# Hybrid trunk on one core: masks made early, fewer VectorE lines per HGRN head, and the S5 half of an output projection in portions between the levels

## The reference

```python
proj = hn @ w_in_even[j]
u, q_b, f_b, i_b, g_b = jnp.split(proj, ...)
y_a = s5_mixer(u, ...)            # gelu, then z * sigmoid(z @ w_glu + b)
y_b = hgrn2_mixer(q_b, f_b, i_b, g_b, lower_bounds[j], hgrn_norm[j])
h = h + jnp.concatenate([y_a, y_b], axis=-1) @ w_out_even[j]

# hgrn2_mixer, per head, in chunks of 64 tokens
k = (1.0 - lbf) * jax.nn.sigmoid(-zf)
b = jnp.cumsum(g_c, axis=2)                     # log decays
o = (q*exp(b)) @ S + (causal q.decay.k) @ v
S_new = exp(b_last) * S + (k*exp(b_last - b)).T @ v
o = o * rsqrt(mean(o*o) + EPS) * head_norm * silu(g)
```

## Time and profile before

| quantity | value |
|---|---|
| median of 3 runs | 2602.95 us (2598.78 to 2605.69) |
| the profiled execution | 2599.74 us |
| its span | 2598.0 us |
| mean granted TensorE clock | 0.971 |
| busy: PE, PEld, DVE, ACT, POOL | 95%, 77%, 46%, 21%, 32% of the span |
| head 0 / heads 1, 2, 3 / last tail | 338 to 378.6 / 378.6 to 465.8 / 465.8 to 484.5 us |
| output projection | 484.5 to 574.8 us |

### The profile page before, as it was taken

One profiled execution on the slowest core, in us unless ns is written; L12 is line 12 of the kernel. 1 busy time (PEld: TensorE's weight loads), 2 busy tenths in 40 slices (PEclk: granted clock), 3 DMA queues, 4 the chain that ended last, 5 costly groups with the idle time before them and its releaser, 6 DMA issues.

```text
span 2598.0 us, 32798 instructions
## 1 busy us (share of the span) xinstructions
PE 2464.0 (95%) x13054; PEld 1998.5 (77%) x13054; DVE 1191.4 (46%) x1229; ACT 548.1 (21%) x850; POOL 833.8 (32%) x493
## 2 busy tenths in 40 slices
PE   8999946899999999999997999989999999999997
PEld 6887745688888888888885776668888888888885
DVE  6886388432432422424617355652432332424625
ACT  3110424311001011011212145632001001011215
POOL 3421442133333333333322244552333333333321
PEclk9999967999999999999998999999999999999998
DMA  7372421211111111111212211021111111111211
GB/s 209 101 115 73 144 68 34 98 49 49 49 48 48 46 46 48 47 48 48 65 49 85 53 25 57 17 73 49 49 46 47 47 47 48 48 48 49 65 49 65
DMA packets 248296, 159.19 MB, mean 61 GB/s; under 512 B 31524, under 2 KB 235400, under 8 KB 248200
## 3 DMA queue, kind: packets, MB, share of 16 engines
q1 hardware_dynamic: 233224, 133.79, 17.9%
q10 hardware_dynamic: 14992, 24.25, 3.5%
HBM read 131.67 MB, written 25.17 MB: 60 GB/s over the span
## 4 chain that ended last, share of the span: by engine, by line
PE 86%; DVE 9%; issue 2%; ACT 2%; POOL 1%; DMA 0%; ACTq 0%; POOLq 0%; DVEq 0%; SPq 0%
PE ps L596 70%; PE ps L1075 3%; PE ps L747 2%; PE ps L1107 2%; PE ps L1035 1%; DVE hg_queries_keys L1849 1%; PE ps L1048 1%; PE ps L1059 1%; PE ps L663 1%; PE ps L768 1%; DVE stage L1519 1%; ACT x_hi L1158 1%; PE ps L783 1%; DVE s_state L1589 1%; DVE stage L1589 1%
## 5 line engine op out<-in xcount | busy, mean ns | idle before, releaser
L450 POOL CAST w_hi<-w_raw 128x1024 fp32r<-128x1024 f32 x198 | 213.0, 1076 | 1499.6 <-PE ps L596 1222.5
L596 PE MATMUL ps<-x_hi,w_hi 128*128 128x512 f32 x1600 | 496.6, 392 | 6.4 <-issue 3.2
L596 PE MATMUL ps<-x_lo,w_hi 128*128 128x512 f32 x1600 | 493.3, 389 | 0.0
L596 PE MATMUL ps<-x_hi,w_lo 128*128 128x512 f32 x1600 | 493.0, 389 | 0.0
L452 POOL TENSOR_TENSOR w_lo<-w_raw,w_hi 128x1024 fp32r<-128x1024 f32 x198 | 487.7, 2463 | 15.8
L596 PE MATMUL ps<-mid_hi,w_hi 128*128 128x512 f32 x1216 | 376.1, 391 | 8.6 <-DVE mid_lo L1908 5.8
L596 PE MATMUL ps<-mid_lo,w_hi 128*128 128x512 f32 x1216 | 375.3, 390 | 0.0
L596 PE MATMUL ps<-mid_hi,w_lo 128*128 128x512 f32 x1216 | 375.2, 390 | 0.0
L596 PEld LDWEIGHTS ps<-x_hi,w_hi 128*128 128x128 f32 x1600 | 299.9, 188 | 73.2 <-issue 8.8
L596 PEld LDWEIGHTS ps<-x_lo,w_hi 128*128 128x128 f32 x1600 | 300.7, 188 | 62.9
L596 PEld LDWEIGHTS ps<-x_hi,w_lo 128*128 128x128 f32 x1600 | 300.6, 188 | 62.7
(11 more groups left out here) (288 smaller groups left out, 2488.7 us busy)
## 6 DMA issues: line engine op xcount, KB each, us to landing
w_raw<-w_mlp_in_in SPq DMA_DIRECT2D x64, 512.0 KB, 4.0
w_raw<-w_mlp_out_in SPq DMA_DIRECT2D x64, 512.0 KB, 4.0
w_raw<-w_in_even_in SPq DMA_DIRECT2D x20, 512.0 KB, 4.0
residual_dram<-residual ACTq DMA_DIRECT2D x2, 4096.0 KB, 13.0
fqig_dram<-stage ACTq DMA_DIRECT2D x16, 512.0 KB, 2.7
w_raw<-w_ple_gate_in SPq DMA_DIRECT2D x16, 512.0 KB, 4.0
x_tokens<-x_in SPq DMA_DIRECT2D x8, 512.0 KB, 7.3
w_raw<-w_out_even_in SPq DMA_DIRECT2D x8, 512.0 KB, 4.1
```

The costliest lines, as they stand in the source:

```text
L450: pool.tensor_copy(WH[:, b, :], RAW[:, b, :]).then_inc(S["w_hi_done"], 1)
L596: ins = pe.matmul(acc[:, h, :], w[:, k, :], x[:, k0 + k, h * HALF:(h + 1) * HALF], start=(k == 0 and w is wh and x is xh), stop=(k == kts ...
```

## The change

- **Masks.** GpSimd makes them right behind slab 3, in a staging buffer, with the same instructions (the block mask as a fifth plane). ScalarE's queue stores them to DRAM; SP loads the diagonal blocks and the block mask back, 5 small DMAs, behind the S5 outputs. `near_masks` only clears `ATD` and waits.
- **Fewer VectorE lines.** `keys` is gone: ScalarE multiplies the keys by `keep`, and the token factor of the values is applied by `value_copy`, now four activations of 128x128 with a per-partition scale (eight small transposes beside the S5 preparation make it a column). `mean_square` is gone: ScalarE's Ln reads PSUM with scale and bias. `near` is 4 instructions of both halves, `attend` 1 per half. For that, banks are dealt anew: near 4, 5; direct 6, 7; transposes and squares both share bank 2, so each waits for the copy of the one before.
- **S5 half first.** The output projection is split by depth. The S5 half (192 matmuls of 512 columns) runs through bank 3 as 16 portions of 12 matmuls. After each of the 14 slots of `hd` = 1 to 4 TensorE runs `FILL` = 4 of them, until they are spent (slot 5 of `hd` = 4). Before portion j it waits for ScalarE's copy of portion j-1. ScalarE copies each at a fixed place of its list (`parts`) and stores it to DRAM. Four slabs of 512 KB with half the depth and twice the width feed it, split by GpSimd behind each head's work.
- **After the heads.** SP restores the residual and the stored part tile by tile, 16 DMAs of 512 KB, 8 MB in all, and only then loads slabs 28 and 29. GpSimd adds the part to the residual (`add_out_part`), three tiles before slab 28, two before slab 29, three after it. The HGRN half runs as 8 units of 24 matmuls.

```diff
             for s in range(2, 4):
                 one(s, s - 1)
-            run(4, 4, 16)
-            one(20, 19)
-            pool.wait_ge(S["s5_y_done"], 8)
+            pool.wait_ge(S["sumsq_ready"], 1)
             own(pool.memset(FULL[:, :, :], 1.0))
...
+            run(4, 4, 16)
+            one(20, 19)
             one(21, 20)
...
+                if hd:
+                    one(SLAB["out"] + hd + 1, 4 * hd, "opart_done")
+            one(SLAB["out"] + 5, 16, "opart_done")
+            def add_out_part(m):
+                pool.wait_ge(tile_loaded[m], 16 * 3)
+                pool.tensor_tensor(H[:, m, :], H[:, m, :], OPART[:, m, :], ALU.add).then_inc(S["out_part"], 1)
+            for m in range(KT):
+                add_out_part(m)
+                if m in (2, 4):
+                    one(SLAB["out"] + 5 + m // 2, UNIT["out"] + m, "acc_done")
...
+            for b in range(2):
+                sp.wait_ge(spilled[b], 16 * (10 + KT))
+            for m in range(KT):
+                sp.dma_start(H[:, m, :], h_dram[m * P:(m + 1) * P, :]).then_inc(tile_loaded[m], 16)
+                sp.dma_start(OPART[:, m, :], part_dram[m * P:(m + 1) * P, :]).then_inc(tile_loaded[m], 16)
+            out_half(1, 2)
+            out_half(1, 3)
...
+            def out_first():
+                pe.wait_ge(S["mid_ready"], 8)
+                for m in range(KT):
...
+                    for h in range(2):
+                        if m + h:
+                            pe.wait_ge(S["opart_copied"], 2 * m + h)
+                        for k in range(4):
+                            for w, x in ((wh, XBh), (wh, XBl), (wl, XBh)):
+                                ins = pe.matmul(PS[:, 3, :], ...)
+                                yield
...
                         if now:
                             level(hd, l, half)
+                        if hd:
+                            dense(first, FILL)
...
-                fn(KQ[:, p, 1, half * HALF:(half + 1) * HALF], FR[:, p, half, :], ACT.Sigmoid, scale=-1.0)
+                own(fn(k, FR[:, p, half, :], ACT.Sigmoid, scale=-1.0))
+                fn(k, k, ACT.Identity, scale=keep[:, hd:hd + 1])
...
+            def parts(hd, slot):
+                while copied[0] < 2 * KT and 12 * (copied[0] + 1) <= FILL * (2 * LEVELS * (hd - 1) + slot + 1):
+                    j = copied[0]
+                    act.wait_ge(S["opart_done"], j + 1)
+                    fn(o, PS[:, 3, :], ACT.Copy).then_inc(S["opart_copied"], 1)
+                    act.wait_ge(S["opart_copied"], j + 1)
+                    act.dma_start(part_dram[...], o).then_inc(spilled[m % 2], 16)
...
+            for hd in range(1, HEADS + 1):
+                key_copy(tail, 0)
+                parts(hd, 0)
+                key_copy(tail, 1)
+                if now:
+                    gate(hd)
+                parts(hd, 5)
+                if hd < HEADS - 1:
+                    for half in range(2):
+                        forget(hd + 1, half)
+                parts(hd, 6)
+                for half in range(2):
+                    squares(tail, half)
+                    if now:
+                        value_copy(hd, half)
+                    parts(hd, 8)
+                act.preload_act_table_set("natural_log_exp_and_others")
+                for half in range(2):
+                    head_rstd(tail, half)
+                    parts(hd, 10 + half)
+                if now:
+                    direct_copy(hd, 0)
+                    parts(hd, 12)
+                    direct_copy(hd, 1)
+                parts(hd, 13)
+                for half in range(2):
+                    y_high(tail, half)
...
             def block_decays(hd):
+                dve.wait_ge(S["hg_f_made"], 2 * hd + 2)
```

More of the change, by code:

```diff
@@ L41 @@
 LAG = 2
+FILL = 4
 V_STEP = 12
@@ L903, in _ @@
             pe.wait_ge(S["mid_ready"], 8)
-            one(22, 24, XB)
-            one(23, 25, XB)
-            run(24, 26, 6, XB)
+            pe.wait_ge(S["opart_copied"], 16)
+            for m in range(KT):
+                u = UNIT["out"] + m
+                if m % 2 == 0:
+                    pe.wait_ge(S["w_ready"], SLAB["out"] + 4 + m // 2 + 1)
+                pe.wait_ge(*free_of(u - 2))
+                wh, wl = out_weights(m)
+                unit(ACC[m % 2], wh, wl, XBh, XBl, kts=4, k0=4)
             def mlp(name, norm, mid0):
@@ L1111, in wo_first @@
                                 yield
-            def dense(work, count):
-                for _ in range(count):
-                    next(work, None)
             pe.wait_ge(S["ss_read"], 4)
@@ L1373, in _ @@
                     if now:
-                        gate(hd)
-                    if hd < HEADS - 1:
-                        for half in range(2):
-                            forget(hd + 1, half)
-                    for half in range(2):
-                        squares(tail, half)
-                        if now:
-                            value_copy(hd, half)
-                    act.preload_act_table_set("natural_log_exp_and_others")
-                    for half in range(2):
-                        head_rstd(tail, half)
-                elif HEADS > 1:
-                    for half in range(2):
-                        forget(1, half)
@@ L1394, in _ @@
+                if now:
+                    direct_copy(hd, 0)
+                    parts(hd, 12)
+                    direct_copy(hd, 1)
+                parts(hd, 13)
+                for half in range(2):
+                    y_high(tail, half)
+            assert copied[0] == 2 * KT
             finish(1, "mlp", 0)
@@ L1914, in _ @@
             for half in range(2):
-                keys(0, half)
                 query_decay(0, half)
@@ L1942, in _ @@
                         if l == 3:
-                            for half in range(2):
-                                near(hd, half)
+                            near(hd)
                     if hd == 0:
@@ L1957, in _ @@
                             forget_in(nxt, half)
-                    if hd and l in (4, 5):
-                        mean_square(tail, l - 4)
                     if nxt < HEADS and l == 4:
-                        for half in range(2):
-                            keys(nxt, half)
                         block_decays(nxt)
@@ L2057, in embed @@
                 end_norm()
[L2059 to L2060 removed]
+            for b in range(2):
+                dve.wait_ge(spilled[b], 16 * (10 + KT))
+            residual(UNIT["out"], 1, ("mlp", 0), None, parts=True)
             mlp("mlp0", 1, 8, (2, ("ple", 0)))
```

171 lines of the change are left out of this document (101 added, 70 removed).

## The result

The changed kernel takes 2614.0 us, median of 5 runs (2609.97 to 2617.53), against 2598.8 us for the kernel before on the same chip: a ratio of 1.0048, 95% interval 1.0031 to 1.0066. It is slower by half a per cent, where 0.6% faster was forecast. The profiled execution took 2617.53 us (span 2615.7), which is 17.7 us of span above the one of before.

The account below looks back on a forecast made before the run. TensorE alone was taken to bound the output projection, a relay with VectorE the fuller partner the heads. +1.0 - 4.2 + 0.7 + 20.0 + 1.0 - 35.3 = -16.8 us gave a median of 2586 us, range 2563 to 2603.

Parts of the forecast that it names:

- start, GLU slab, head 0: Ahead of head 1: masks +1, second GLU slab without its wait -4.2, head 0 +0.7 us; together -2.5.
- heads 1 to 3: Heads 1 to 3 with portions: 35.4, 38.3 and 33.7 us, 107.4 for 87.2, so +20 us.
- last tail: Tail behind the heads: portions and shared bank 2 cost, one VectorE hop goes; +1 us (0 to +5).
- output projection: Output projection with half its matmuls, a 6.5 us slab stall ahead of unit 4: 90.3 becomes 55.0, -35.3 us.
- with the portions it is 30.4 ... so TensorE becomes the bound: Heads 1 to 3: TensorE's own 17.7 us a head becomes 30.4, above all VectorE sums, so TensorE bounds them.
- Waits for bank 3: Heads 1 to 3: TensorE waits for ScalarE's portion copies, 5.0, 7.9 and 3.3 us by head.
- the upper end: Heads 1 to 3: every wait half as long again and a half clock after the long ones, +32 us.
- GpSimd's splits slow VectorE's two-input lines: In the heads: four GpSimd splits of 3.4 us each slow VectorE, inside the ends given, with TensorE the bound.
- pays nothing there: Heads 1 to 3: VectorE's removed lines, about 5 us a head, save nothing because TensorE is the bound.
- The lower-clock one: Rival: bank waits keep TensorE at its lower clock through the heads; heads and tail +68, 2633 us; chance 9%.
- It decides from +46 on: Heads and tail: from +46 us on, the result counts for the rival of TensorE's lower clock level, chance 9%.
- The third: Rival: worse waits, or VectorE and TensorE alternate instead of overlapping; heads and tail +34, 2599 us; chance 13%.

Follow-up runs that it names:

- e1: The changed kernel without the portions, the output projection whole behind the heads: 2599.5 us, ratio 1.0003 to the kernel before.
- e8: The changed kernel with whole portions of 12 matmuls between the two halves of a pass: 2607.1 us, ratio 1.0026 to the kernel before.
- e3: The changed kernel with each portion whole, 12 matmuls behind a pass's second half: 2584.8 us, ratio 0.9940 to the kernel before.
- e6: The changed kernel with eight matmuls behind each pass's second half instead of four behind each half: 2604.5 us, ratio 1.0015 to the kernel before.
- e2: The changed kernel without TensorE's wait for bank 3 and without ScalarE's copies of the portions: 2593.2 us, ratio 0.9973 to the kernel before.
- e7: The changed kernel with eight matmuls behind each second half, no bank 3 wait and no ScalarE copies: 2580.6 us, ratio 0.9923 to the kernel before.
- e5: The changed kernel with GpSimd's first two projection splits held until head 0's block decays are made: 2615.9 us, ratio 1.0056 to the kernel before.
- c2: The changed kernel with whole portions in slots 1, 5, 7, 13, last two slabs ahead of the restore, late first splits: 2578.6 us, ratio 0.9917.
- c3: c2 with the stored half added by VectorE instead of GpSimd: 2579.7 us, ratio 0.9927 to the kernel before.

## Why the prediction was wrong

The sum of the prediction was -16.8 us and the spans say +17.7. Term by term, in us (the measured ones add up to +16.5; 1.2 us lie behind the output projection):

| term | forecast | measured | off by |
|---|---|---|---|
| start, GLU slab, head 0 | -2.5 | +1.6 | 4.1 |
| heads 1 to 3 | +20 | +43.9 | 23.9 |
| last tail | +1 | +4.0 | 3.0 |
| output projection | -35.3 | -33.0 | 2.3 |

**The step that failed is "with the portions it is 30.4 ... so TensorE becomes the bound".** It took a stage in which two engines hand work to each other and, because one's sum was the larger, let the other's share vanish; and its 30.4 us of TensorE's time a head had nothing in them for the lower clock or for the small pieces. The forecast of the three heads was 91.2 us of matmuls and 16.2 of waits for bank 3. Measured are 104.4 busy and 26.7 idle:

- *Waits for bank 3*: forecast 16.2, measured 16.8. Following ScalarE's list was right in sum (4.7, 8.3 and 3.9 us by head, forecast 5.0, 7.9 and 3.3), and seven of the eight waits stand at the slots that it gave. In head 2 the sum came out with some luck: slot 7 waited 4.28 us instead of 6.0, and 2.30 at slot 1 were not forecast.
- *Other idle time of TensorE*: forecast 0, measured 26.7 - 16.8 = 9.9, of which 5.1 are waits for VectorE's updates and 3.9 stand ahead of the sums of squares, in e1 too. The prediction had said that the four matmuls between the halves delay the update each time, and then charged nothing for it. e8 against e3 shows what that place costs, 23.3 us for whole portions, and e6 against the changed kernel 11.0 for fours, there together with the number of pieces.
- *Busy time*: forecast 91.2, measured 104.4. About 8 of these 13.2 us are the lower clock behind the bank waits (e2: 8.2 less busy for the same matmuls). I had it only in the upper end. The rest can be the 0.28 instead of 0.226 us a matmul in pieces of four; 168 of them would by these two figures be 9 us, more than the 5 that are left, so this share is an estimate.

So of the 23.7 us between 107.4 and 131.1, 13.2 are busy time, 9.9 idle time that had no term, and 0.6 the waits for the bank. The table of e6 and e7 divides the start of the projection another way: 25 us for the waits with their clock and 11 for place and size of the pieces. The other 12 us (498.0 against e1's 485.7) are what e7 still pays for its 192 matmuls.

**Head 0 and the GLU.** TensorE's wait for the slab went as forecast and the last matmuls of the GLU ended near 333, but VectorE made the block decays in 10.6 instead of 2.4 us, and TensorE waited 11.5 us for the first update. GpSimd's instructions beside them, its two splits and the products behind, did that: without them the six took 1.65 us in e5. I had "GpSimd's splits slow VectorE's two-input lines" for the heads and not for this place. What that cost at the end of head 0 is open, for e5 only moved it to other lines. What sets the changed kernel back against the one before is seen later. By its fourth update the changed kernel is ahead of the one before, 358.82 against 359.88; the fifth comes at 367.70 against 366.37. Between the two stand TensorE's wait and VectorE's idling behind it:

```profile
365.86 1.09 PE L888 MATMUL ps<-identity,hg_v 128*128 128x128 f32 x4 [7.80 <-ACT hg_v_tokens L1232]
...
367.70 1.22 DVE L1949 TENSOR_TENSOR hg_queries_keys<-hg_queries_keys,hg_block_decay 128x1024 f32<-128x1024 f32 x1 [2.97 <-PE ps L864]
```

`value_tokens` of the second half (L888) needs the bank that the first half has filled, now bank 2 for both, and ScalarE's copy stands in its list behind a line of the GLU that VectorE finishes late. The level behind it (L864) starts at 366.88 instead of 361.15. e1 and e5 have the same 7.8 us and the same 8.9 us between the two updates (6.5 before). The prediction had a term for this bank in the tail and none in head 0. No run gives the two halves two banks again, so this is read from the chain and not tested.

**Tail.** e1 has +2.1 of the +4 without any portion, where the new wait is that for the shared bank 2; the portions have the other 2. Mis-sized, within the range given for it (0 to +5).

**Output projection.** Right in its mechanism: the order behind the restore, the stall, its releaser. The landing and the stall were each within 1.5 us; the 1.36 us for VectorE were not in the sum.

**VectorE's lines.** That their saving "pays nothing there" no run tests with the portions in place. Without them it pays at most 2.7 us (e1), since with the one bank for transposes and squares 9.0 us of waits for ScalarE stand in place of 14.8 for VectorE.

**The rivals.** None had the result. The lower-clock one had its direction and a part of its mechanism, and by its own rule ("It decides from +46 on") the 48 us of heads and tail fall to it; but it had 68, and the clock's share is about 8 us, not 54. The third, "VectorE and TensorE alternate instead of overlapping", had the other part of the mechanism and with +34 too little for it. The clock rival's ground was in part misread: the start "at half clock after idle stretches of 4 to 6 us" is in the earlier trace rows, but the earlier trace rows has no start at half clock: there two matmuls together take 0.73 us, where they take 1.22 in the earlier trace rows. The lower level comes a good 1 us later, and its last pair starts at 325.19. TensorE's timeline before:

```profile
322.43 0.62 PE L783 MATMUL ps<-mid_lo,w_hi 128*128 128x512 f32 x2
...
323.49 1.05 PE L783 MATMUL ps<-mid_hi,w_hi 128*128 128x512 f32 x2
...
326.77 0.62 PE L783 MATMUL ps<-mid_lo,w_hi 128*128 128x512 f32 x2
```

"TensorE idles less when it is busier" held: the mean clock in the heads rose from the earlier trace rows's 0.80, 0.65 and 0.83 to 0.89, 0.86 and 0.92. By the Trainium skill's rule on cycling through PSUM banks (TensorE: Matmul & The Clock Gate, "A second HAM failure mode: psum-queue depth-cycling") throughput falls through a swing of the clock; here the swing is there, the matmuls behind the two longest waits for the bank run at the lower level, and without the waits (e2) the clock is 0.97 against 0.89, but by the 8.2 us of busy time it is a third of their price.

The idea of the change was sound, its arrangement wasn't. Moved whole, and to where they stand beside an update, the same 192 matmuls put off the start of the output projection by 12.0 us over e1 instead of 48.4 (c2), and the kernel is 0.8% faster than before.

## What to carry to other kernels

When work is put into the holes of a relay between two engines, don't add busy times: ask for each piece whether the other engine waits for it (between the parts of a stage) or works beside it (behind the stage's last part), because that decides more than the piece's length. Give a piece the size of its result buffer and put other work between two pieces, so that the copy that frees the buffer is never waited for; here 16.8 us of such waits came with another 8.2 us of busy time at the lower clock. And a hole at the front of a stretch is worth only what is left of it at the stretch's end: the 10.5 us that e5 won in head 0 were 1.4 at head 1, because the work that it moved slowed other lines instead.

## What the runs showed of the hardware

**Short VectorE instructions with two inputs from SBUF pay for each instruction of GpSimd beside them.** The six products of 128x256 down to 128x8 elements took 1.65 us in e5 and 10.56 in the changed kernel, where GpSimd ran one instruction after the other. In the output projection of c2 VectorE's line with two inputs from SBUF took 3.23 us beside GpSimd's three additions and 1.28 after them, while the line between them, which reads PSUM, took the same 1.22 or 1.23 in both. VectorE and GpSimd in c2:

```profile
522.71 1.22 DVE L2067 TENSOR_TENSOR residual<-ps,residual 128x1024 f32 x1 [0.63 <-DVE stage L1622]
525.60 3.23 DVE L1628 SCALAR_TENSOR_TENSOR x_lo<-residual,vectors,x_hi  x1 [1.67 <-ACT x_hi L1231]
528.76 3.41 DVE L1622 TENSOR_TENSOR stage<-stage,stage 128x1024 f32<-128x1024 f32 x1
532.50 1.23 DVE L2067 TENSOR_TENSOR residual<-ps,residual 128x1024 f32 x1 [0.33 <-DVE stage L1622]
535.39 1.28 DVE L1628 SCALAR_TENSOR_TENSOR x_lo<-residual,vectors,x_hi  x1 [1.67 <-ACT x_hi L1231]
```

```profile
525.38 9.00 POOL L551 TENSOR_TENSOR residual<-residual,out_part 128x1024 f32<-128x1024 f32 x3
```

In c3, without the additions, L1628 took 1.28 or 1.29 us in four of its six places of that stage, and 3.14 and 2.07 in the two where a split of GpSimd lay beside it (523.93 and 546.77). The Trainium skill has the rule (SBUF — State Buffer, "Who interferes with whom"): a VectorE instruction with two SBUF inputs contends with a GpSimd instruction that reads SBUF, and the port pair that they share is an exclusive lock, held by whoever issues first. The traces agree: 1 to 2.5 us for products that take 0.2 to 0.4 alone, about the length of the GpSimd instruction beside them (1.23 to 2.70 us). Moving GpSimd's work earlier or later is therefore not free for VectorE even where nobody waits for GpSimd: e5 is the case of it.
